# The sixteen gate columns of a first projection: split f32r products replaced by f32 products in four column groups, one block ahead

## The chip, the cores and the metric

The kernel runs on one core of a Trainium2 chip. Its time is device microseconds of one execution; a kernel is judged by the median of its runs. One execution was also taken by the profiler, and all rows below come from that one.

## The reference: what is computed

One layer of a streaming encoder on a prompt of 4096 frames and 8 running streams of 16 new frames (128 sample rows). Only the beginning matters here:

```
xn   = rms_norm(h, ln_g)                     # 1024 columns
proj = xn @ w_in
qkv_a, a_raw, b_raw, ... = split(proj)       # 1536 | 8 | 8 | ...
conv = silu(depthwise causal conv, width 4, of qkv_a)
beta = sigmoid(b_raw)
g    = -exp(a_log) * softplus(a_raw + dt_bias)
gc   = cumsum(g) within blocks of 64 frames
```

The sixteen columns a_raw and b_raw are the gate columns. The delta rule, an attention over a band of frames, an output projection and an embedding follow.

## The kernel before

The kernel is a sequence of stages, each with its own buffers and semaphores and a barrier at its end. The first is `project_a` (line 110), which makes the 1536 columns of qkv_a and the 16 gate columns; the second, `project_b`, makes the other columns and reads back what the first has stored. Each engine has its own program, written out by hand in `project_a`, and runs it in order; semaphores (`wait_ge`, `then_inc`) are the only links.

**Tiling.** The 4096 prompt frames and 128 sample rows are 33 row tiles of 128. A block b is two tiles, 256 frames, so there are 16 full blocks, and block 16 holds the sample tile alone. Each tile is squared and scaled on ACT, transposed on PE (`transposes`), multiplied by ln_g on DVE into `x_full` (two buffers), and split into a high f32r part on ACT (`split_hi`) and the rest on DVE (`split_lo`). The tiles of block b+1 are prepared during block b: the first around groups 0 to 4, the second around groups 5 to 9.

**Products.** The 1536 columns are twelve groups g of 128. A group is a `product` (line 484): for each of 8 slices of the 1024 rows, three f32r matmuls (`matmul3`, lines 86 to 90: high by high, low by high, high by low), 24 in all, into one of four PSUM banks `psG`. After the twelve groups of a block the gate columns are a thirteenth `product` of 24 matmuls with 16 columns of weights, into columns 0 to 255 of the bank `psAB` (line 533). The weights themselves arrive in 32 pieces in block 0 and before, and are split likewise: the high part on ACT (`hi_part`), the low part alternately on DVE and POOL (`lo_part`, line 214). In block 0 group 9 waits for pieces 24 to 31.

**Behind the products.** ACT copies each group into one of six `raw` buffers (line 438), DVE convolves it with four instructions (lines 573 and 576), and ACT applies SiLU (line 394). For block b-1, PE makes four key-query products during block b, one behind each of the groups 0 to 3 (`keys_queries`, line 501); each goes into the one bank `psK`, must be copied by ACT (`take_kq`, line 401, one of two `kq` buffers) before the next, and is stored by SP (`store_kq`, line 240). `take_kq` for the third waits until the stores of the first have landed. Behind group 5 PE makes the query sums in columns 256 to 511 of `psAB` (`query_sums`, line 509).

**Gate arithmetic.** `decays(b)` (line 578) is at the end of DVE's block b: it adds dt_bias to the gate product, and ten more steps on 16x256 tiles, most of which wait for the one before, give gc and beta. ACT's part, two exponentials and a logarithm (lines 464 to 468), is at the end of ACT's block. Both engines go on to the next block's groups only behind it.

**Queue.** SP issues every DMA of the stage in order. In block b it stores the key-query products of b-1, loads and stores row tiles, then `store(b)` (line 249): it waits for the last SiLU, stores the block, waits for the end of `decays(b)`, and stores gc and beta with four DMAs (line 256).

Of the kernel before, what the change touches and what calls it, by code (L numbers as in the profile page):

```python
# [26 lines left out]
F32R = mybir.dt.float32r  # L27
ACT = mybir.ActivationFunctionType
ALU = mybir.AluOpType
AX = mybir.AxisListType  # L30

P = 128
# [77 lines left out]
def project_a(nc, d, s):  # L110
# [4 lines left out]
    G = QKV // P  # L115
    HA, N, HALO, TAPS = s.HA, 2 * P, s.CONVW - 1, s.CONVW
    C = s.DV
    WCOLS = QKV + 2 * HA
    PAIRS = HA // 2
    RING, SLOTS = 6, 7  # L120
    CUTS = [0, 3 * P, 6 * P, 9 * P, WCOLS]
    PIECES = [(k, CUTS[i], CUTS[i + 1]) for i in range(4) for k in range(KT)]
    WIDEST = max(b - a for k, a, b in PIECES)
    HALVES = len(PIECES) // 2
    with ExitStack() as stack:
        ph = Phase(nc, stack)
        w_hi = ph.sb("a_w_hi", [P, KT, WCOLS], F32R)
        w_lo = ph.sb("a_w_lo", [P, KT, WCOLS], F32R)
        x_raw = [ph.sb(f"a_x{i}", [P, D]) for i in range(2)]
        squares = ph.sb("a_squares", [P, D], mybir.dt.bfloat16)  # L130
        x_full = [ph.sb(f"a_x_full{i}", [P, KT, P]) for i in range(2)]
# [7 lines left out]
        ssq_rows = ph.sb("a_ssq_rows", [P, N])  # L139
        pair_ones = ph.sb("a_pair_ones", [P, 32])  # L140
        taps = ph.sb("a_taps", [P, TAPS, G])
        lnT = ph.sb("a_lnT", [P, KT])
        ident = ph.sb("a_ident", [P, P])
        ssq = ph.sb("a_ssq", [P, 2])
# [16 lines left out]
        psK = ph.ps("a_psK", [P, 512])  # L161

        ln_in = ph.sem("a_ln_in")
        consts = ph.sem("a_consts")
        filled = ph.sem("a_filled")
        cleared = ph.sem("a_cleared")
# [31 lines left out]
        stored = [ph.sem(f"a_stored{i}") for i in range(2)]  # L198
        ab_stored = ph.sem("a_ab_stored")
        last_rows = ph.sem("a_last_rows")  # L200
        V_AB, S_AB = 11, 3

        stage = [act[1][:, :, :].rearrange("p g n -> p (g n)")[:, i * WIDEST:(i + 1) * WIDEST] for i in range(SLOTS)]

        def tiles_of(b):
            return range(2 * b, min(2 * b + 2, TILES))
# [16 lines left out]
        def _(sp):  # L223
# [6 lines left out]
            def spill(t):  # L230
                sp.wait_ge(full_ok, t + 1)
                sp.dma_start(d.xT[t], x_full[t % 2][:, :, :]).then_inc(spilled[t % 2], 16)
# [16 lines left out]
            def store(b):  # L249
                sp.wait_ge(silu, G * (b + 1))  # L250
                sp.dma_start(d.qkvB[b], act[b % 2][:, :, :]).then_inc(stored[b % 2], 16)
                sp.wait_ge(ab_v, V_AB * (b + 1))
                n = N // C
                for x, there in ((gc[0:HA, :], d.gcC), (beta[HA:2 * HA, :], d.betaC)):
                    for e in range(2):
                        sp.dma_start(there[n * b:n * (b + 1), e * PAIRS:(e + 1) * PAIRS].rearrange("n h i -> h n i"),
                                     x[e::2, :].rearrange("h (n i) -> h n i", n=n)).then_inc(ab_stored, 16)
# [5 lines left out]
            for m, (k, a, b) in enumerate(PIECES):  # L263
                if m >= SLOTS:
                    weights_ready(sp, m - SLOTS + 1)
                sp.dma_start(stage[m % SLOTS][:, 0:b - a], d.w_in[k * P:(k + 1) * P, a:b]).then_inc(w_in[m % SLOTS], 16)
                if m == 5:
                    with nc.allow_non_contiguous_dma(reason="small per-channel constants, once"):
                        for j in range(TAPS):
                            sp.dma_start(taps[:, j, :], d.conv_w[j, :].rearrange("(g p) -> p g", p=P)).then_inc(consts, 16)  # L270
                        sp.wait_ge(cleared, 2)
                        sp.dma_start(dt_b[0:HA, :], d.dt_bias.rearrange("(h o) -> h o", o=1)).then_inc(consts, 16)
                        sp.dma_start(alog[0:HA, :], d.a_log.rearrange("(h o) -> h o", o=1)).then_inc(consts, 16)
                if m == 16:
                    load_x(2)
                    spill(0)
                if m == 20:
                    load_x(3)
                    spill(1)
            for b in range(BLOCKS + 1):  # L280
                if b:
                    for f in range(4):
                        store_kq(b - 1, f)
                for t in tiles_of(b + 1):
                    if t + 2 < TILES:
                        load_x(t + 2)
                    spill(t)
                    if b and t % 2 == 0:
                        store_rows(b - 1)
                if b == BLOCKS:  # L290
                    store_rows(b - 1)
                else:
                    store(b)
            with nc.allow_non_contiguous_dma(reason="three columns, once"):
                sp.wait_ge(halo_ok, G * BLOCKS)
                sp.dma_start(d.lastT.rearrange("(g p) t -> p g t", p=P), halo[:, :, :]).then_inc(last_rows, 16)
# [71 lines left out]
        def _(e):  # L368
# [10 lines left out]
            def split_hi(t):  # L379
                b, a = t // 2, t % 2  # L380
                e.wait_ge(full_ok, t + 1)
                if b >= 2:
                    e.wait_ge(grp_ok, G * (b - 1))
                    e.wait_ge(ab_ok, b - 1)
                e.activation(xT_hi[b % 2][:, :, a * P:(a + 1) * P], x_full[a][:, :, :], ACT.Copy).then_inc(hi_ok, 1)

            def hi_part(m):
# [15 lines left out]
            def take_rows(b):  # L403
                e.wait_ge(rows_ps, b + 1)
                if b:
                    e.wait_ge(rows_out, 16 * PAIRS * b)
                e.activation(ssq_rows[:, :], psAB[:, N:], ACT.Copy).then_inc(rows_ok, 1)

            square(0)
            square(1)  # L410
# [12 lines left out]
            for b in range(BLOCKS + 1):  # L423
                ahead = list(tiles_of(b + 1))
                for g in range(G):
# [29 lines left out]
                    if len(ahead) > 1:  # L455
                        if g == 5:
                            square(ahead[1])
                        if g == 6:
                            scale(ahead[1])
                        if g == 9:  # L460
                            split_hi(ahead[1])
                if b < BLOCKS:
                    conv_silu(b, G - 1)
                e.wait_ge(ab_v, V_AB * b + 3)
                e.activation(u[:, :], na[:, :], ACT.Exp).then_inc(ab_s, 1)
                e.activation(en[:, :], xa[:, :], ACT.Exp, scale=-1.0).then_inc(ab_s, 1)
                e.wait_ge(ab_v, V_AB * b + 4)
                e.activation(ln_w[:, :], w[:, :], ACT.Ln).then_inc(ab_s, 1)

        @block.tensor  # L470
        def _(pe):
# [10 lines left out]
            def product(out, cols, b, n, first):  # L482
# [4 lines left out]
                                   xT_lo[b % 2][:, k, 0:n], k == 0, k == KT - 1)  # L487
                return last

            def keys_queries(b, f):  # L490

                a, x = f // 2, act[b % 2]
                n = 4 * b + f
                pe.wait_ge(silu, G * b + 2 * PAIRS)
                if n:
                    pe.wait_ge(kq_ok, n)
                rows_e = slice(f % 2 * C, (f % 2 + 1) * C)
                for p in range(PAIRS):
                    for c2 in range(2):
                        at = slice(a * P + c2 * C, a * P + (c2 + 1) * C)  # L500
                        last = nc.tensor.matmul(psK[c2 * C:(c2 + 1) * C, p * 2 * C:(p + 1) * 2 * C], x[rows_e, PAIRS + p, at],
                                                x[rows_e, p:p + PAIRS + 1:PAIRS, at], start=True, stop=True)
                last.then_inc(kq_ps, 1)

            def query_sums(b):
                pe.wait_ge(qsq_ok, b + 1)
                pe.wait_ge(ab_v, V_AB * b + 1)
                for p in range(PAIRS):
                    last = nc.tensor.matmul(psAB[32 * p:32 * (p + 1), N:], pair_ones[:, :], qsq[:, p, :], start=True, stop=True)
                last.then_inc(rows_ps, 1)  # L510
# [3 lines left out]
            for b in range(BLOCKS + 1):  # L514
# [3 lines left out]
                for g in range(G):  # L518
# [5 lines left out]
                        keys_queries(b - 1, g)  # L524
                    if b and g == 5:
                        query_sums(b - 1)
                    if g == 3 and ahead:
                        transposes(ahead[0])
                    if g == 8 and len(ahead) > 1:
                        transposes(ahead[1])  # L530
                if b:
                    pe.wait_ge(rows_ok, b)
                product(psAB[0:2 * HA, 0:n], slice(QKV, WCOLS), b, n, None).then_inc(ab_ok, 1)

        @block.vector
        def _(v):
# [11 lines left out]
            def full(t):  # L548
                v.wait_ge(xT_ps, t + 1)
                if t >= 2:  # L550
                    v.wait_ge(spilled[t % 2], 16 * (t // 2))
                    v.wait_ge(lo_ok, t - 1)
                v.tensor_tensor(x_full[t % 2][:, :, :], psT[:, :].rearrange("p (k n) -> p k n", k=KT),
                                lnT[:, :].unsqueeze(2).to_broadcast([P, KT, P]), ALU.mult).then_inc(full_ok, 1)

# [22 lines left out]
            def decays(b, gates):  # L578
                at = V_AB * b
                n = P * len(tiles_of(b))  # L580
                v.wait_ge(ab_ok, b + 1)
                v.tensor_scalar(xa[:, 0:n], psAB[0:2 * HA, 0:n], dt_b[:, :], None, ALU.add).then_inc(ab_v, 1)
                v.wait_ge(ab_v, at + 1)
                v.tensor_scalar(nx[:, :], xa[:, :], -1.0, None, ALU.mult).then_inc(ab_v, 1)
                v.wait_ge(ab_v, at + 2)
# [33 lines left out]
            for b in range(BLOCKS):  # L619
# [3 lines left out]
                for g in range(G):  # L623
# [8 lines left out]
                        full(ahead[1])  # L632
                    if g == 9 and len(ahead) > 1:
                        split_lo(ahead[1])
                decays(b, gate)
            decays(BLOCKS, gate_s)


GROUPS = 4
# [2618 lines left out]
```

## Time and profile before

| | |
|---|---|
| Median of 3 runs | 3945.96 us (3920.86 to 3954.39) |
| Profiled execution, its own time | 3943.41 us |
| Its span | 3941.6 us |
| Mean granted TensorE clock | 0.945 |
| Busy: PE, DVE, ACT, POOL | 3548.4, 2212.2, 1299.6, 1018.9 us |
| `project_a` | 0 to 803.8 us |

Busy time is the share in which an engine had an instruction running. Matmuls are pipelined, so the start-to-start spacing, not the duration, is what one costs. A line number is that of kernel.py; a helper's line covers all its callers. SPq is SP's DMA queue.

### The profile page before, as it was taken

What the parts mean: (1) busy time and instruction counts of PE and PEld (TensorE: products, weight loads), DVE (VectorE), ACT (ScalarE), POOL (GpSimd) and SP (SyncE); (2) the same over time, 40 slices, a digit from 0 to 9 for tenths busy, and PEclk for the clock granted to TensorE, in tenths of its full rate; (3) what the DMA queues carried; (4) which work ended last, traced back from release to release, by engine and by line L of the source; (5) the groups of instructions that cost most, each with busy time, mean ns of one, the idle gap of its engine ahead of it and who ended that gap; (6) DMA issues with size and microseconds to landing.
All of it is one profiled execution on the core that took longest, in us unless ns stands there. A gap on an engine that the chain in (4) does not pass through costs nothing. (4 is left out here: it accounts for less than half of the span.)

```text
span 3941.6 us, 68538 instructions
## 1 busy us (share of the span) xinstructions
PE 3548.4 (90%) x26510; PEld 3020.0 (77%) x26510; DVE 2212.2 (56%) x4204; ACT 1299.6 (33%) x2368; POOL 1018.9 (26%) x1284
## 2 busy tenths in 40 slices
PE   7999999979996898995777569999977999999999
PEld 6999999967885686874676467888854788888887
DVE  7777777357974758681466436666633423333332
ACT  5455444232222323211233206666622211111111
POOL 4222222057983525400577600000000000000000
PEclk9999999889998899997899779999988999999999
DMA  5333433244334333333999522222244312112120
GB/s 157 104 118 101 115 100 102 60 147 158 115 112 140 118 116 116 111 109 79 211 231 233 131 62 92 77 73 81 84 117 167 106 59 69 64 57 69 65 67 34
DMA packets 380768, 426.62 MB, mean 108 GB/s; under 512 B 188267, under 2 KB 271499, under 8 KB 377918
## 3 DMA queue, kind: packets, MB, share of 16 engines
q1 hardware_dynamic: 380486, 422.80, 37.8%
q8 instruction: 185, 3.03, 0.3%
q14 instruction: 97, 0.79, 0.1%
HBM read 265.09 MB, written 160.25 MB: 108 GB/s over the span
## 5 line engine op out<-in xcount | busy, mean ns | idle before, releaser
L88 PE MATMUL b_psP<-b_w_hi,b_xT_hi 128*128 128x512 f32 x1320 | 525.5, 398 | 105.8 <-DVE b_xT_lo L1180 89.0
L89 PE MATMUL b_psP<-b_w_lo,b_xT_hi 128*128 128x512 f32 x1320 | 522.6, 396 | 0.0
L90 PE MATMUL b_psP<-b_w_hi,b_xT_lo 128*128 128x512 f32 x1320 | 521.6, 395 | 0.0
L88 PE MATMUL a_psG<-a_xT_hi,a_w_hi 128*128 128x256 f32 (+1 forms) x1632 | 475.0, 291 | 10.3 <-DVE a_xT_lo L559 9.4
L90 PE MATMUL a_psG<-a_xT_hi,a_w_lo 128*128 128x256 f32 (+1 forms) x1632 | 467.0, 286 | 0.0
L89 PE MATMUL a_psG<-a_xT_lo,a_w_hi 128*128 128x256 f32 (+1 forms) x1632 | 466.8, 286 | 0.0
L88 PEld LDWEIGHTS b_psP<-b_w_hi,b_xT_hi 128*128 128x128 f32 x1320 | 253.5, 192 | 166.1 <-DVE b_xT_lo L1180 112.8
L88 PEld LDWEIGHTS a_psG<-a_xT_hi,a_w_hi 128*128 128x128 f32 x1632 | 316.5, 194 | 26.6 <-DVE a_xT_lo L559 9.8
L576 DVE SCALAR_TENSOR_TENSOR a_act<-a_raw,a_taps,a_act 128x256 f32<-128x256 f32 x576 | 308.7, 536 | 20.5
L90 PEld LDWEIGHTS a_psG<-a_xT_hi,a_w_lo 128*128 128x128 f32 x1632 | 317.1, 194 | 0.0
L89 PEld LDWEIGHTS a_psG<-a_xT_lo,a_w_hi 128*128 128x128 f32 x1632 | 316.7, 194 | 0.0
L90 PEld LDWEIGHTS b_psP<-b_w_hi,b_xT_lo 128*128 128x128 f32 x1320 | 253.3, 192 | 53.8
L89 PEld LDWEIGHTS b_psP<-b_w_lo,b_xT_hi 128*128 128x128 f32 x1320 | 253.6, 192 | 52.6
L2516 DVE CUSTOM_DVE_ANT_0 f_neg<-f_score,f_bias 128x640 f32<-128x640 f32 (+4 forms) x256 | 192.4, 780 | 83.5 <-PE f_score L2416 55.2
L3000 POOL TENSOR_SCALAR h_var<-h_ssq 128x1 f32<-128x1 f32 x33 | 6.3, 190 | 870.8 <-ACT h_squares L3032 870.8
L88 PE MATMUL h_psH<-h_w_hi,h_mT_hi 128*128 128x512 f32 x528 | 209.2, 396 | 6.7 <-DVE h_w_lo L107 6.7
L1180 DVE TENSOR_TENSOR b_xT_lo<-b_x_full,b_xT_hi 128x1024 fp32r<-128x1024 f32 x72 | 105.7, 1468 | 186.2 <-ACT b_xT_hi L1095 186.2
L900 DVE TENSOR_TENSOR b_tmp_v<-b_M,b_col_v 128x62 f32<-128x62 f32 (+28 forms) x464 | 205.9, 484 | 3.5
L1143 ACT ACTIVATE b_rows<-b_psP 128x512 f32<-128x512 f32 x99 | 58.8, 598 | 451.5 <-PE b_psP L90 316.7
L2335 ACT ACTIVATE f_prob<-f_neg,f_low 128x640 f32<-128x640 f32 (+4 forms) x256 | 201.2, 788 | 17.9 <-DVE f_low L2516 17.9
L90 PE MATMUL h_psH<-h_w_hi,h_mT_lo 128*128 128x512 f32 x528 | 206.4, 391 | 0.0
L89 PE MATMUL h_psH<-h_w_lo,h_mT_hi 128*128 128x512 f32 x528 | 206.4, 391 | 0.0
(378 smaller groups left out, 7707.8 us busy)
## 6 DMA issues: line engine op xcount, KB each, us to landing
rows_b<-b_rows SPq DMA_DIRECT2D x165, 256.0 KB, 2.1
b_x_full<-xT SPq DMA_DIRECT2D x72, 512.0 KB, 4.1
qkvB<-a_act SPq DMA_DIRECT2D x16, 1536.0 KB, 5.1
d_conv_T<-qkvB SPq DMA_DIRECT2D x32, 768.0 KB, 5.8
xT<-a_x_full SPq DMA_DIRECT2D x33, 512.0 KB, 5.1
h_mixed<-mixed SPq DMA_DIRECT2D x33, 512.0 KB, 4.0
out<-h_y SPq DMA_DIRECT2D x33, 512.0 KB
a_x<-in_x_prompt SPq DMA_DIRECT2D x32, 512.0 KB, 4.4
```

Of the source, the lines that this page charges most:

```text
L88: nc.tensor.matmul(out, x_hi, w_hi, start=first, stop=False)
L89: nc.tensor.matmul(out, x_hi, w_lo, start=False, stop=False)
L90: return nc.tensor.matmul(out, x_lo, w_hi, start=False, stop=last)
L576: v.scalar_tensor_tensor(out, x[:, j:j + N], taps[:, j, g:g + 1], out, ALU.mult, ALU.add).then_inc(conv, 1)
L900: eng.tensor_tensor(t, U[:, c0:c1, j:j + 1].to_broadcast([P, c1 - c0, L]), factor.unsqueeze(1).to_broadcast([P, c1 - c0, L]), ALU.mult).th ...
L1143: e.activation(rows[u % ROWS][:, :], psP[u % BANKS][:, :], ACT.Copy if seg == V else ACT.Silu).then_inc(taken, 1)
L1180: v.tensor_tensor(xT_lo[n % XBUFS][:, :, :], x_full[n % 2][:, :, :], xT_hi[n % XBUFS][:, :, :].bitcast(F32), ALU.subtract).then_inc(lo_ok, 1)
L2335: e.activation(prob[h % 4][:, 0:n], neg[h % 2][:, 0:n], ACT.Exp, scale=-1.0, bias=low[a.b][:, h:h + 1], accum_out=total[a.b][:, h:h + 1]). ...
L2516: v.tensor_tensor_reduce(neg[h % 2][:, 0:n], score[h % 2][:, 0:n], bias[:, h, KEYS - n:], -1.0 / ROOT, BIG, ALU.add, ALU.min, low[a.b][:, ...
L3000: g.tensor_scalar(var[:, :], ssq[:, :], 1.0 / D, EPS, ALU.mult, ALU.add).then_inc(e_var, 1)
```

## The change

The gate columns leave the split f32r weights. They get a tile of their own, `w_ab`, 32 columns wide in f32 (the 16 gate columns and the 16 behind them, of which the results are not used), loaded once at weight piece 12. A function `gates(t)` on PE multiplies one row tile in f32 from `x_full`: eight products of 128 streamed columns, of which product q of each four writes the partitions 32q to 32q+15 (and 16 unused) of `psAB`, so that the eight slices of the contraction add up in four parts. DVE adds the four parts with three new adds. All of it is done one block ahead: PE calls `gates` for the tiles of block b+1 behind groups 9 and 11 of block b (and for tiles 0 and 1 behind group 2 of block 0); `decays(b + 1)` stands where `decays(b)` stood, and `decays(0)` behind group 5 of block 0; SP stores the gates of b+1 behind the block b.

```diff
-    WCOLS = QKV + 2 * HA
+    PARTS, PCOLS = 4, 32
-    CUTS = [0, 3 * P, 6 * P, 9 * P, WCOLS]
+    CUTS = [0, 3 * P, 6 * P, 9 * P, QKV]
+        w_ab = ph.sb("a_w_ab", [P, KT, PCOLS])
-        V_AB, S_AB = 11, 3
+        V_AB, S_AB = 10 + PARTS, 3
 # SP
             def store(b):
                 sp.wait_ge(silu, G * (b + 1))
                 sp.dma_start(d.qkvB[b], act[b % 2][:, :, :]).then_inc(stored[b % 2], 16)
+
+            def store_gates(b):
                 sp.wait_ge(ab_v, V_AB * (b + 1))
...
+                if m == 12:
+                    sp.dma_start(w_ab[:, :, :], d.w_in[:, QKV:QKV + PCOLS].rearrange("(k p) c -> p k c", p=P)).then_inc(w_ab_in, 16)
...
+            store_gates(0)
             for b in range(BLOCKS + 1):
...
                     store(b)
+                    if b + 1 < BLOCKS:
+                        store_gates(b + 1)
 # ACT
-                    e.wait_ge(ab_ok, b - 1)
...
+            def decays(b):
+                e.wait_ge(ab_v, V_AB * b + PARTS + 2)
+                (the same two exponentials; wait for + PARTS + 3; the same logarithm)
...
+                    if b == 0 and g == 5:
+                        decays(0)
                 if b < BLOCKS:
                     conv_silu(b, G - 1)
-                e.wait_ge(ab_v, V_AB * b + 3)
-                (two exponentials, wait, logarithm)
+                    decays(b + 1)
 # PE
+            def gates(t):
+                b, at = t // 2, slice(t % 2 * P, (t % 2 + 1) * P)
+                pe.wait_ge(full_ok, t + 1)
+                if t == 0:
+                    pe.wait_ge(w_ab_in, 16)
+                if b:
+                    pe.wait_ge(ab_v, V_AB * (b - 1) + PARTS)
+                if b >= 2:
+                    pe.wait_ge(rows_ok, b - 1)
+                for k0 in range(0, KT, PARTS):
+                    for q in range(PARTS):
+                        last = nc.tensor.matmul(psAB[PCOLS * q:PCOLS * (q + 1), at], w_ab[:, k0 + q, :], x_full[t % 2][:, k0 + q, :],
+                                                start=k0 == 0, stop=k0 + PARTS == KT)
+                last.then_inc(ab_ok, 1)
...
-                pe.wait_ge(ab_v, V_AB * b + 1)
+                pe.wait_ge(ab_v, V_AB * (b + 1) + PARTS)
...
+                    if b == 0 and g == 2:
+                        gates(0)
+                        gates(1)
+                    if g == 9 and ahead:
+                        gates(ahead[0])
+                    if g == G - 1 and len(ahead) > 1:
+                        gates(ahead[1])
...
-                if b:
-                    pe.wait_ge(rows_ok, b)
-                product(psAB[0:2 * HA, 0:n], slice(QKV, WCOLS), b, n, None).then_inc(ab_ok, 1)
 # DVE
                 if t >= 2:
...
+                    v.wait_ge(ab_ok, t - 1)
...
-                v.wait_ge(ab_ok, b + 1)
+                v.wait_ge(ab_ok, tiles_of(b)[-1] + 1)
                 v.tensor_scalar(xa[:, 0:n], psAB[0:2 * HA, 0:n], dt_b[:, :], None, ALU.add).then_inc(ab_v, 1)
+                for q in range(1, PARTS):
+                    v.wait_ge(ab_v, at + q)
+                    v.tensor_tensor(xa[:, 0:n], xa[:, 0:n], psAB[PCOLS * q:PCOLS * q + 2 * HA, 0:n], ALU.add).then_inc(ab_v, 1)
...
+                    if b == 0 and g == 5:
+                        decays(0, gate)
-                decays(b, gate)
-            decays(BLOCKS, gate_s)
+                decays(b + 1, gate if b + 1 < BLOCKS else gate_s)
```

## Rows read from the trace of the kernel before

**Rows 1.** Busy time by stretch: us, PE, PEld, DVE, ACT, POOL, PEclk, DMA, GB/s
```profile
158.75:202.84 44.09, 44.09 (x403) 41.84 (x401) 32.88 (x63) 22.11 (x44) 10.97 (x29) 1.00 0.38 109
749.00:790.00 41.00, 41.00 (x203) 39.90 (x199) 0.00 (x0) 2.81 (x9) 0.00 (x0) 0.51 0.10 14
```

**Rows 2.** Waits of PE, 110 to 700 us: us in total, times, longest us
```profile
PE a_psK L501 <- ACT a_kq L401: 2.0, 4, 0.8
```

**Rows 3.** Timeline of PE, blocks 2 and 3: start, us, engine, line, op, tiles
```profile
156.03 0.28 PE L88 MATMUL a_psAB<-a_xT_hi,a_w_hi 128*16 128x256 f32 x1
...
158.64 0.28 PE L90 MATMUL a_psAB<-a_xT_hi,a_w_lo 128*16 128x256 f32 x1
...
169.79 1.09 PE L501 MATMUL a_psK<-a_act 64*64 64x128 f32 x16
...
173.85 1.09 PE L501 MATMUL a_psK<-a_act 64*64 64x128 f32 x16
...
200.12 0.28 PE L88 MATMUL a_psAB<-a_xT_hi,a_w_hi 128*16 128x256 f32 x1
```

**Rows 4.** Timeline of DVE across the same end of a block
```profile
157.03 1.52 DVE L576 SCALAR_TENSOR_TENSOR a_act<-a_raw,a_taps,a_act 128x256 f32<-128x256 f32 x3
158.95 0.47 DVE L582 TENSOR_SCALAR a_xa<-a_psAB,a_dt 16x256 f32<-16x256 f32 x1 [0.39 <-PE a_psAB L90]
159.46 0.28 DVE L584 TENSOR_SCALAR a_softplus<-a_xa 16x256 f32<-16x256 f32 x1
...
166.71 0.24 DVE L573 TENSOR_SCALAR a_act<-a_raw,a_taps 128x256 f32<-128x256 f32 x1
```

**Rows 5.** Timeline of SP's queue, the same stretch
```profile
166.81 1.34 SPq L256 DMA_DIRECT2D gcC<-a_gc  x2
...
169.46 7.41 SPq L240 DMA_DIRECT2D kq<-a_kq  x8
```

**Rows 6.** Timeline of ACT, the same stretch
```profile
160.32 0.42 ACT L465 ACTIVATE a_u<-a_na 16x256 f32<-16x256 f32 x1
...
168.88 0.58 ACT L401 ACTIVATE a_kq<-a_psK 128x512 f32<-128x512 f32 x1
...
172.88 0.60 ACT L401 ACTIVATE a_kq<-a_psK 128x512 f32<-128x512 f32 x1 [1.80 <-DMA kq<-a_kq]
```

**Rows 7.** Timeline of PE around f32 products (x4: window cut short)
```profile
93.19 0.28 PE L90 MATMUL a_psG<-a_xT_hi,a_w_lo 128*128 128x256 f32 x1
93.40 0.64 PE L509 MATMUL a_psAB<-a_qsq,a_pair_ones 128*32 128x256 f32 x8
...
94.19 0.28 PE L89 MATMUL a_psG<-a_xT_lo,a_w_hi 128*128 128x256 f32 x1
...
93.40 0.42 PE L509 MATMUL a_psAB<-a_qsq,a_pair_ones 128*32 128x256 f32 x4
...
71.20 1.09 PE L501 MATMUL a_psK<-a_act 64*64 64x128 f32 x16
```

**Rows 8.** A PSUM tile as operand on DVE: ns min/median/max, first and last start
```profile
L3116 DVE TENSOR_TENSOR h_pT_lo<-h_psE,h_pT_hi x33: 411/412/416, 3077.1 to 3918.2; 128x256 fp32r<-128x256 f32 x33
```

**Rows 9.** Timeline of DVE and PE in block 0
```profile
52.88 0.34 DVE L573 TENSOR_SCALAR a_act<-a_raw,a_taps 128x256 f32<-128x256 f32 x1
...
58.97 0.39 PE L88 MATMUL a_psG<-a_xT_hi,a_w_hi 128*128 128x256 f32 x1 [0.89 <-DVE a_w_lo L217]
```

**Rows 10.** Timeline of SP's queue at the end of the stage
```profile
791.11 0.38 SPq L298 DMA_DIRECT2D rawT_s<-a_act  x1
...
803.81 0.36 SPq L920 DMA_DIRECT2D b_x_full<-xT  x1
```

**Rows 11.** DMA from 791 to 804 us, in 40 slices
```profile
GB/s 0 0 0 217 296 284 296 284 296 285 295 167 0 0 0 0 0 0 0 0 0 0 0 0 0 0 0 0 0 0 0 0 0 13 13 0 0 0 0 0
```

**Rows 12.** Timeline of PE at its first wide products
```profile
26.75 0.58 PE L88 MATMUL a_psG<-a_xT_hi,a_w_hi 128*128 128x256 f32 x1 [9.42 <-DVE a_xT_lo L559]
...
29.48 0.41 PE L88 MATMUL a_psG<-a_xT_hi,a_w_hi 128*128 128x256 f32 x1
```

More of the change, by code:

```diff
@@ L126, in project_a @@
         ph = Phase(nc, stack)
-        w_hi = ph.sb("a_w_hi", [P, KT, WCOLS], F32R)
-        w_lo = ph.sb("a_w_lo", [P, KT, WCOLS], F32R)
+        w_hi = ph.sb("a_w_hi", [P, KT, QKV], F32R)
+        w_lo = ph.sb("a_w_lo", [P, KT, QKV], F32R)
         x_raw = [ph.sb(f"a_x{i}", [P, D]) for i in range(2)]
@@ L163, in project_a @@
         ln_in = ph.sem("a_ln_in")
+        w_ab_in = ph.sem("a_w_ab_in")
         consts = ph.sem("a_consts")
@@ L407, in take_rows @@
                 e.activation(ssq_rows[:, :], psAB[:, N:], ACT.Copy).then_inc(rows_ok, 1)
+            def decays(b):
+                e.wait_ge(ab_v, V_AB * b + PARTS + 2)
+                e.activation(u[:, :], na[:, :], ACT.Exp).then_inc(ab_s, 1)
+                e.activation(en[:, :], xa[:, :], ACT.Exp, scale=-1.0).then_inc(ab_s, 1)
+                e.wait_ge(ab_v, V_AB * b + PARTS + 3)
+                e.activation(ln_w[:, :], w[:, :], ACT.Ln).then_inc(ab_s, 1)
             square(0)
@@ L461, in _ @@
                             split_hi(ahead[1])
+                    if b == 0 and g == 5:
+                        decays(0)
                 if b < BLOCKS:
                     conv_silu(b, G - 1)
-                e.wait_ge(ab_v, V_AB * b + 3)
[L465 to L468, printed above, removed]
+                    decays(b + 1)
         @block.tensor
@@ L580, in decays @@
                 n = P * len(tiles_of(b))
-                v.wait_ge(ab_ok, b + 1)
+                v.wait_ge(ab_ok, tiles_of(b)[-1] + 1)
                 v.tensor_scalar(xa[:, 0:n], psAB[0:2 * HA, 0:n], dt_b[:, :], None, ALU.add).then_inc(ab_v, 1)
+                for q in range(1, PARTS):
+                    v.wait_ge(ab_v, at + q)
+                    v.tensor_tensor(xa[:, 0:n], xa[:, 0:n], psAB[PCOLS * q:PCOLS * q + 2 * HA, 0:n], ALU.add).then_inc(ab_v, 1)
+                at += PARTS - 1
                 v.wait_ge(ab_v, at + 1)
```

## The prediction, made before the changed kernel was run

> **What bounds the kernel now.** The change touches only the first stage, project_a, which ends near 803.8 us of the 3941.6 us span, so I read that stage. First the busy time by stretch: one full block (two row tiles, 256 frames) lasts 44.09 us, and in it PE is busy for all 44.09, DVE for 32.88, ACT for 22.11, with a granted clock of 1.00 [rows 1]. PE looks like the only bound. Then the waits of PE: between 110 and 700 us, 2.0 us in all, each of them for ACT's copy of a key-query product, a_kq [rows 2]. They are few, but the same copy is what becomes late if anything else slips, so I followed one block through PE, DVE, ACT and SP in order of time.
>
> I call E the moment at which PE has started the last of a block's twelve wide groups and begins the gate product: E = 156.03. The gate product is 24 instructions, the last at 158.64. The next block's third key-query product starts at 169.79, its fourth at 173.85, and the next E is 200.12 [rows 3]. So a period is 17.82 us (E to the fourth product) plus 26.27 us (from there to the next E).
>
> Beside the first part runs a chain that the gate product does not set. DVE ends the twelfth convolution at 158.55, that is E + 2.5; starts the gate arithmetic at 158.95 after a wait of 0.39; and begins the next convolution at 166.71 [rows 4]. SP cannot store the gates before that: its issues run from 166.81, and the key-query stores queued behind them from 169.46 [rows 5]. ACT may reuse its copy buffer only when the first of these stores has landed, so its third copy starts at 172.88 after a wait of 1.80 for that DMA and ends at 173.48; its second copy, held by the first convolution after the gate arithmetic, ends at 169.46 [rows 6]. PE needs them at 173.85 and 169.79: the slack is 0.37 and 0.33 us. So in each block two bounds lie within 0.4 us of each other: PE's own work, and the chain E, twelfth convolution, gate arithmetic, SP's gate stores, key-query store, ACT copy. The 2.7 us of gate product run in the shadow of that chain.
>
> **The change part by part.**
>
> Removed on PE: the 24 narrow instructions between E and the next block. They go from 156.03 to 158.75 (158.64 and one spacing of 0.11): 2.72 us [rows 3].
>
> Added on PE: two calls of gates per block, each 8 f32 products of 32 columns on 128 rows, streaming 128. The query sums are the nearest kind (32 columns, four column groups): 4 products appear as 8 records. The first four records together last 0.42 us while a single one lasts 0.40, so the four groups run side by side. From the last wide record before them (93.19) to the second after (94.19) is 1.00 us where 0.24 is normal, two spacings of 0.12: 0.76 us for 8 x 256 streamed columns [rows 7]. A call of gates has 16 records x 128 columns, the same total: I take 0.8 us. The upper end is the key-query product, 16 records x 128 columns in two column groups, which lasts 1.09 [rows 7] and costs about 1.2 with the same entry and exit. I take 0.8 because width, group count and streamed columns match the sums. The page "TensorE: Matmul & The Clock Gate" of the Trainium skill (What happens when you issue a matmul) says that, without hardware decode, each matmul instruction costs about 62 ns of sequencer time; by that a call would be 16 x 62 = 1.0 us and 0.2 of entry, 1.2 in all. The four starts within 0.02 us speak against it here.
>
> Where these calls lie matters. The first sits behind group 9, inside the 26.27 us, where nothing waits: +0.8 per block on the period. The second sits behind E, in the shadow of the chain: nothing. If the chain were gone, both would count, with the 2.72 saved.
>
> Added on DVE: three adds of a 16x256 PSUM part, each waiting for the one before. An add with one PSUM operand on 256 columns lasts 0.41 [rows 8]; dependent steps of this arithmetic follow each other every 0.50 us (158.95 to 159.46) [rows 4]. I take 0.50 each, 1.5 in all; ends are 0.41 each without a gap and 0.65. Against it stands the 0.39 wait for the gate product, which goes, and about 0.1 with which unrelated DVE instructions overlap: the arithmetic can start at about E + 2.45. Net delay of its end against E: 1.5 - 0.5 = +1.0 us (0.7 to 1.5). ACT's exponential now starts at 160.32 [rows 6], right behind its input, so it moves along.
>
> Queued behind it: on DVE the next block's convolutions, on ACT the next group's copies, on SP four gate stores and then the key-query stores. All end 1.0 later against E. The fourth product then starts at E + 17.45 + 1.0 + 0.15 = E + 18.6, where PE alone would be ready at E + 0.8 + 15.1 = E + 15.9. So E to the fourth product grows from 17.82 to 18.6, and PE now waits some 2.7 us per block before the second, third and fourth products. Per period: +0.8 (chain) +0.8 (first call) = **+1.6 us**, for the 14 periods between the fourth product of block 1 and that of block 15: **+22.4**. The gates of the last, half-wide tile need adds of 128 columns, about 0.35 each: +0.5 and again +0.8, **+1.3**.
>
> Block 0: it now does the arithmetic twice, once behind group 5 and once at its end. The added one takes the 7.76 us from 158.95 to 166.71 plus 1.5, that is 9.3 us, on DVE before the convolution that now starts at 52.88. DVE shows no idle time from there on, and the low parts of the weights for groups 9 to 11 are queued behind: PE already waits 0.89 for them at 58.97 [rows 9]. Nothing covers it: +9.3. Then the block's ordinary arithmetic is 1.5 longer, of which about 0.6 is hidden by ACT's table load: +0.9. The two calls for tiles 0 and 1 vanish in PE's wait. Together **+10.2** (7 to 12).
>
> SP: its gate stores move from the block's own to the next one's values, same number and place. The extra load of the 16 columns at weight piece 12 is one issue of perhaps 1.5 us at a time when SP waits for DVE: nothing, up to 1. In block 0 the loads of tile 4 come some 15 us later, and its rows are used only in block 1.
>
> The end of the stage: E of the last block, the gate product, DVE's arithmetic, two stores, and the next stage's first load is issued at 803.81. After the change only the copy of rawT_s is left, issued at 791.11; its bytes flow until slice 12 of 40 in the window from 791 to 804, that is 794.9 [rows 10, 11]. Nothing else is open, so the next stage starts near 795.3: **-8.5** (-7 to -9).
>
> Sum: 22.4 + 1.3 + 10.2 - 8.5 = **+25.4 us**. The profiled execution took 3943.4, so 3968.8; it stands 2.6 below the median of the three runs, whose spread is 33 us. I predict 3970.
>
> **The rivals.**
> 1. The saving reaches the end. If the chain did not hold PE, a period would lose 2.72 - 1.6 = 1.1 us: 16 x 1.1 = 18 less, 8.5 less at the end, 10.2 more in block 0: -16, 3927, and -26, 3917, if DVE's doubled arithmetic in block 0 were covered too. It decides only if the fourth product can start before E + 17.0, that is if the arithmetic ended 0.5 us earlier against E than now; with three more adds it cannot, and the four waits of PE in [rows 2] show the chain already touching. Chance 0.06.
> 2. The new waits lower TensorE's clock. Before its first wide product PE stood 9.42 us; that product and those up to 29.48 last 0.41 and more where 0.28 is usual, the half clock (1.2 GHz) by their length: 2.7 us at half speed, 1.4 lost [rows 12]. In the last, half-wide block the granted clock fell to 0.51 with PE never idle [rows 1]. If each block's three waits (0.8, 1.9, near 0) did this once: 15 x 1.4 = +21, 3990. Against: a block has waited before, and from 158.75 to 202.84 the clock was 1.00. The same page of the Trainium skill (HAM oscillation) says that a product stream broken by waits falls back to half clock again and again, which is this case; no row here shows it. Chance 0.14.
> 3. Everything dear: a call of gates at 1.2 (+0.4 per period) and adds at 0.65 (+0.45): +13, and block 0 at 12: 3984. Chance 0.15.
> 4. The forecast, +18 to +33: 0.65.
>
> **How the numbers follow.** Likeliest 3970. The range goes from 3946 (adds and block 0 at their low ends: +15, less 12 for the scatter of a median of such runs) to 4000 (rivals 2 and 3 with some scatter). One per cent, 39 us, is about what a measurement of this kernel can tell from no change. The forecast case lies under it in most of its width (0.54 of 0.65), rival 3 by half, rival 2 hardly; rival 1 is within it except for scatter: faster 0.03, same 0.70, slower 0.27.
>
> **What would show it.** In the profile after: PE idle before the second and third key-query products, 1 to 2 us each, released by ACT a_kq; periods between fourth products of 45.5 to 46 us where they are 44.1; gates as 16 records in about 0.55 us, and the adds 0.50 apart; 8 to 10 us of PE idle in block 0 before group 9's last weights, released by DVE a_w_lo; the next stage's first load within 5 us of the last ACT copy. Wrong if PE's idle time in blocks 2 to 15 stays under 0.5 us per block (then the chain does not hold, rival 1), if the granted clock falls under 0.95 there (rival 2), or if block 0 gives back what the arithmetic costs it.

## The result, and the profile after

The changed kernel takes 3993.24 us (median of 6, 3983.42 to 4007.91) where the kernel before takes 3944.49 (3920.86 to 3954.39): ratio 1.0136, 95% interval 1.0099 to 1.0173. It is slower by 49 us; 25 were forecast for the likeliest case.

The whole difference lies in project_a. The next stage's first load, at 803.81 before [rows 10], is at 852.46, 48.65 later. The profiled execution of the changed kernel took 4007.9 us, 64.5 more than the profiled one before: some 16 us of that lie behind this stage. The medians differ by 48.75 us, so I take those 16 us as scatter between executions; that is not shown.

Timeline of PE in block 3 of the changed kernel, the counterpart of [rows 3] (start, us, then as before):

```profile
163.78 0.28 PE L90 MATMUL a_psG<-a_xT_hi,a_w_lo 128*128 128x256 f32 x1
163.99 0.65 PE L515 MATMUL a_psAB<-a_x_full,a_w_ab 128*32 128x128 f32 x16
...
164.79 0.28 PE L89 MATMUL a_psG<-a_xT_lo,a_w_hi 128*128 128x256 f32 x1
...
170.50 0.65 PE L515 MATMUL a_psAB<-a_x_full,a_w_ab 128*32 128x128 f32 x16
...
178.82 1.09 PE L530 MATMUL a_psK<-a_act 64*64 64x128 f32 x16 [0.53 <-ACT a_kq L409]
...
184.76 1.09 PE L530 MATMUL a_psK<-a_act 64*64 64x128 f32 x16 [1.79 <-ACT a_kq L409]
...
186.47 0.28 PE L90 MATMUL a_psG<-a_xT_hi,a_w_lo 128*128 128x256 f32 x1
186.59 0.38 PE L88 MATMUL a_psG<-a_xT_hi,a_w_hi 128*128 128x256 f32 x1
186.77 0.42 PE L89 MATMUL a_psG<-a_xT_lo,a_w_hi 128*128 128x256 f32 x1
...
190.34 1.09 PE L530 MATMUL a_psK<-a_act 64*64 64x128 f32 x16
```

E is 170.39 here. The two new waits stand before the second and third key-query products, and 1.8 us after the third begins the wide products go over from 0.12 to 0.21 us apart. The third starts at E + 14.4, where 14.6 follows from the forecast's chain. The fourth starts at E + 19.95; in the period in which the clock stays up and no further wait is added it starts at E + 18.5, where 18.6 was forecast. Below are the waits of PE from 120 to 740 us, where [rows 2] had 2.0 us from 110 to 700, and the granted clock (PEclk, third from the end) in the stretch of the slow products, in the next, and in the last block:

```profile
PE a_psK L530 <- ACT a_kq L409: 31.5, 29, 1.8
```

```profile
138.80:142.20 3.40, 3.40 (x18) 3.40 (x18) 1.70 (x4) 0.76 (x2) 0.41 (x2) 0.51 0.84 147
142.30:183.00 40.70, 40.15 (x375) 37.77 (x374) 30.05 (x57) 18.63 (x37) 9.71 (x27) 1.00 0.34 105
790.00:845.00 55.00, 55.00 (x274) 53.17 (x274) 0.82 (x1) 4.16 (x13) 0.00 (x0) 0.50 0.11 16
```

DVE and SP behind the twelfth convolution, against [rows 4, 5]:

```profile
172.86 0.47 DVE L616 TENSOR_SCALAR a_xa<-a_psAB,a_dt 16x256 f32<-16x256 f32 x1
173.36 1.32 DVE L619 TENSOR_TENSOR a_xa<-a_xa,a_psAB 16x256 f32<-16x256 f32 x3
174.72 0.28 DVE L622 TENSOR_SCALAR a_softplus<-a_xa 16x256 f32<-16x256 f32 x1
...
181.88 0.24 DVE L607 TENSOR_SCALAR a_act<-a_raw,a_taps 128x256 f32<-128x256 f32 x1
```

```profile
181.97 1.34 SPq L260 DMA_DIRECT2D gcC<-a_gc  x2
...
184.62 5.31 SPq L242 DMA_DIRECT2D kq<-a_kq  x6
```

The three adds take 1.36 us. The arithmetic starts at E + 2.5, and the next convolution at E + 11.5, 0.8 later against E than before.

PE in block 0, and the end of the stage:

```profile
61.37 0.90 PE L492 MATMUL a_psT<-a_ident,a_x 128*128 128x128 f32 x3 [5.49 <-ACT a_x L386]
61.41 0.24 DVE L607 TENSOR_SCALAR a_act<-a_raw,a_taps 128x256 f32<-128x256 f32 x1
```

```profile
846.68 0.39 SPq L307 DMA_DIRECT2D rawT_s<-a_act  x1
847.11 0.68 SPq L309 DMA_DIRECT2D gcT<-a_gc  x1
847.83 1.12 SPq L310 DMA_DIRECT2D betaT<-a_beta  x1
852.46 0.35 SPq L959 DMA_DIRECT2D b_x_full<-xT  x1
```

By the starts of the fourth key-query products the 48.65 us divide up:

| from | to | before | after | difference | forecast |
|---|---|---|---|---|---|
| start | block 1 | 85.70 | 95.79 | +10.1 | +10.2 |
| block 1 | block 15 (14 periods) | 619.48 | 657.55 | +38.1 | +22.4 |
| block 15 | block 16 | 42.98 | 48.67 | +5.7 | +1.3 |
| block 16 | rawT_s | 42.95 | 44.67 | +1.7 | 0 |
| rawT_s | next stage | 12.70 | 5.78 | -6.9 | -8.5 |

Of the 14 periods, the ten in which the clock fell last 47.26 to 47.29 us; the four others last 46.18, 45.77, 46.82 and 46.03. The waits before the second and third products are the same in all 14 (0.52 to 0.54 and 1.77 to 1.79 us), so their length does not tell why the clock fell in ten. Three of the four others have one more wait for a_kq, of 0.18 to 0.99 us, before the fourth product; the kernel before has such odd waits in four periods too, and its 14 periods last 44.25 on average.

### The profile page after: what moved, and what is told of

Same layout as the page of the kernel before. It is cut to its first block and busy times, and to the rows that moved or that the text cites. A ratio compares the mean times of both kernels' runs of the same rounds, so it can differ in the third digit from the quotient of the medians.

```text
span 4006.1 us, 68894 instructions
## 1 busy us (share of the span) xinstructions
PE 3573.1 (89%) x26630; PEld 3040.2 (76%) x26630; DVE 2228.1 (56%) x4255; ACT 1296.2 (32%) x2369; POOL 1007.7 (25%) x1284
## 5 line engine op out<-in xcount | busy, mean ns | idle before, releaser
L88 PE MATMUL a_psG<-a_xT_hi,a_w_hi 128*128 128x256 f32 (+1 forms) x1632 | 493.6, 302 | 9.5 <-DVE a_xT_lo L593 9.4
L89 PE MATMUL a_psG<-a_xT_lo,a_w_hi 128*128 128x256 f32 (+1 forms) x1632 | 480.7, 295 | 0.0
L90 PE MATMUL a_psG<-a_xT_hi,a_w_lo 128*128 128x256 f32 (+1 forms) x1632 | 480.1, 294 | 0.0
L88 PEld LDWEIGHTS a_psG<-a_xT_hi,a_w_hi 128*128 128x128 f32 x1632 | 332.1, 204 | 32.7 <-issue 11.7
L89 PEld LDWEIGHTS a_psG<-a_xT_lo,a_w_hi 128*128 128x128 f32 x1632 | 332.8, 204 | 0.0
L90 PEld LDWEIGHTS a_psG<-a_xT_hi,a_w_lo 128*128 128x128 f32 x1632 | 332.7, 204 | 0.0
L610 DVE SCALAR_TENSOR_TENSOR a_act<-a_raw,a_taps,a_act 128x256 f32<-128x256 f32 x576 | 309.3, 537 | 20.5
L88 PE MATMUL h_psG<-h_w_hi,h_hT_hi 128*128 128x512 f32 x528 | 205.7, 390 | 0.0
```

The lines of the kernel that those rows point to most:

```text
L88: nc.tensor.matmul(out, x_hi, w_hi, start=first, stop=False)
L89: nc.tensor.matmul(out, x_hi, w_lo, start=False, stop=False)
L90: return nc.tensor.matmul(out, x_lo, w_hi, start=False, stop=last)
L610: v.scalar_tensor_tensor(out, x[:, j:j + N], taps[:, j, g:g + 1], out, ALU.mult, ALU.add).then_inc(conv, 1)
```

## The experiments

All ratios are to the kernel before on the same chip; medians of kernels measured on different chips are compared only roughly. Periods are between fourth key-query products; the stage end is the next stage's first load.

| kernel | median, us | ratio (95%) | usual period | clock falls, blocks 2 to 15 | stage end |
|---|---|---|---|---|---|
| before | 3944.49 | 1 | 44.09 | none | 803.8 |
| after | 3993.24 | 1.0136 (1.0099 to 1.0173) | 47.27 | 10 | 852.5 |
| fill | 3975.25 | 1.0075 (1.0044 to 1.0106) | 45.77 | none | 841.4 |
| no_adds | 3967.10 | 1.0070 (1.0046 to 1.0094) | 45.0 or 46.5 | 6 | 829.4 |
| one_slice | 3958.72 | 1.0042 (1.0017 to 1.0066) | 43.9 to 47.0 | 9 | 824.1 |
| three_steps | 3967.66 | 1.0072 (1.0052 to 1.0092) | 45.12 | none | 822.7 |
| late | 3919.37 | 0.9952 (0.9926 to 0.9978) | 43.98 | none | 777.2 |
| late0 | 3915.48 | 0.9946 (0.9922 to 0.9971) | 43.98 | none | 775.0 |
| before_late | 3918.03 | 0.9955 (0.9931 to 0.9979) | 44.09 | none | 777.4 |
| last_fill | 3922.39 | 0.9958 (0.9938 to 0.9978) | 44.09 | none | 783.3 |
| late3 | 3907.84 | 0.9918 (0.9886 to 0.9950) | 43.36 | none | 768.3 |
| late3_pitch | 3908.94 | 0.9919 (0.9890 to 0.9949) | 43.14 | none | 763.3 |
| late3_shift | 3905.49 | 0.9908 (0.9875 to 0.9942) | 43.36 | none | 768.5 |

**fill**: do the waits lower the clock, or the f32 products?

```diff
+                    if b and g in FILL:        # FILL = {1: 4, 2: 12}
+                        pe.wait_ge(evac, G * b + g - 2)
+                        for _ in range(FILL[g]):
+                            nc.tensor.matmul(psG[(g + 1) % 4][:, 0:n], w_hi[:, 0, (g + 1) * P:(g + 2) * P],
+                                             xT_hi[b % 2][:, 0, 0:n], start=True, stop=True)
```

> The changed kernel, but PE does not stand idle before the key-query products: 4 extra wide products before the second and 12 before the third of each block (about 0.5 and 1.4 us of streaming, into a PSUM bank that the next group resets). The results are unchanged, there is only more work. Theory (the waits lower TensorE's clock): the granted clock stays 1.00 in blocks 2 to 15, the period falls from 47.3 to 45.8 us, the stage ends 15 to 25 us sooner than in the changed kernel, the kernel is 0.4 to 0.6% faster than the changed one (about 3973, +0.7% on before). Rival (the f32 products in column groups lower the clock, or the length of the period is work on PE): the clock keeps falling once per block, periods stay 47.3 or grow by up to 1.9 us: 3993 to 4020.

```profile
110.00:720.00 610.00, 600.80 (x5611) 567.67 (x5610) 454.12 (x872) 285.46 (x568) 135.20 (x385) 1.00 0.36 103
```

The window's row has the clock at 1.00 with more work done. The usual period is 45.77, the forecast's 45.7; five of the 14, with an odd wait of 0.54 to 1.17 us, are longer, and the 14 together last 645.4 us where the changed kernel's last 657.6: 12.2 less. The stage ends 11 us earlier, less than expected, since in block 16 the clock fell again, at 775.5, and its period came out 1.9 longer than in the changed kernel. The f32 products in column groups do not lower the clock; the waits do.

**no_adds**: the changed kernel with its `for q in range(1, PARTS)` loop replaced by `v.sem_inc(ab_v, PARTS - 1)`. It leaves out three of the four parts of each gate.

> The changed kernel without the three adds: only the first of the four parts enters the gates (this part of the computation is left out), everything else in its place. Theory (the chain from the last group over DVE's gate arithmetic to the ACT copies sets the fourth key-query product): the arithmetic ends 1.36 us sooner, all of it reaches PE while it still waits (2.3 us per block now): period 45.8 - 1.3 = 44.5, and since the third product's wait shrinks to about 0.5 us the clock may hold 1.00, which gives 1.5 more against 47.3. Stage end 35 to 45 us before that of the changed kernel; 3950 to 3960. Rival (adds are hidden beside PE): period unchanged at 47.3, 3993.

```profile
132.95 1.09 PE L530 MATMUL a_psK<-a_act 64*64 64x128 f32 x16 [1.62 <-ACT a_kq L409]
```

The period is 45.0 instead of the expected 44.5 where the clock holds, and the clock falls in six periods. The stage ends 23 us before that of the changed kernel, not 35 to 45. The adds reach PE, but only 0.8 of their 1.36 us: with them gone, ACT's exponential waits for its table load again, which in the kernel before ends at 160.31, just before the start in [rows 6]. The rival, no change, is out. In blocks 2 to 15 there is one wait of 1.6 us before the third product here, and none before the second: one such wait is enough for the clock to fall in some blocks.

**one_slice**: the kernel before with an eighth of the gate product; the other seven slices are left out.

```diff
-                product(psAB[0:2 * HA, 0:n], slice(QKV, WCOLS), b, n, None).then_inc(ab_ok, 1)
+                matmul3(nc, psAB[0:2 * HA, 0:n], w_hi[:, 0, QKV:WCOLS], w_lo[:, 0, QKV:WCOLS], xT_hi[b % 2][:, 0, 0:n],
+                        xT_lo[b % 2][:, 0, 0:n], True, True).then_inc(ab_ok, 1)
```

> The kernel before with 3 instead of 24 narrow gate products per block (7 of 8 slices of the contraction are left out), everything else in its place. Theory (the gate product runs in the shadow of the chain): E to the fourth key-query product can shrink only by the slack, so the period goes from 44.09 to about 43.5, not to 41.7; PE begins to wait about 1.8 us per block for a_kq, and the clock may fall as in the changed kernel, which would make it 44 to 45. Time between -10 and +15 us on before. Rival (PE's work is the bound): period 41.7, 2.4 us less in each of 16 blocks, -40 us, 3905.

```profile
PE a_psK L501 <- ACT a_kq L401: 29.1, 28, 1.8
```

This is the sharpest of them: 2.4 us less PE work per block make the kernel slower (1.0042). PE now waits 29.1 us between 120 and 700 us, and the clock falls in nine periods. Of the five periods without a fall, three last 43.9, only 0.2 less than before, and two, with a further wait of 1.0 us, last 45.0.

**three_steps**: the kernel before, with 1.36 us more on DVE alone.

```diff
+                for q in range(1, 4):
+                    v.wait_ge(ab_v, at + q)
+                    v.tensor_tensor(xa[:, 0:n], xa[:, 0:n], xa[:, 0:n], ALU.min).then_inc(ab_v, 1)
```

> The kernel before with three extra dependent 16x256 steps on DVE behind the first of the gate arithmetic (minimum of a tile with itself; results unchanged), 0.45 us each; PE, ACT and SP do the same as before. Theory: 1.36 us on a chain with 0.35 us of slack gives +1.0 per period, 45.1, with the clock at 1.00 if waits of about 1 us do not lower it: +15 to +17 us, 3960; with a fall of the clock in most blocks up to +38. Rival (DVE's steps are hidden, PE is the bound): no change, 3944.

```profile
172.40 1.09 PE L501 MATMUL a_psK<-a_act 64*64 64x128 f32 x16 [0.97 <-ACT a_kq L401]
```

The usual period grows by 1.03 us, as expected, and this wait of 0.97 us does not lower the clock in a full block. In four periods a second wait of 0.28 to 1.17 us follows within 6 us, and there the clock stays up too.

**late, late0, before_late**: only the steps that read PSUM stay at the block's end. Late and late0 start from the changed kernel, before_late from the kernel before. On DVE (on ACT and SP alike; in before_late `finish(b - 1)`):

```diff
                 for g in range(G):
                     convolve(b, g)
...
+                    if g == 5:
+                        finish(b, gate)        # the ten steps behind the PSUM reads
-                decays(b + 1, gate if b + 1 < BLOCKS else gate_s)
+                gather(b + 1)                  # the four steps that read psAB
```

> The changed kernel, but of the gate arithmetic only the four steps that read the PSUM bank stay at the end of a block; the other ten (with ACT's three activations, and SP's gate stores) move behind group 5 of the next block, where no key-query product follows. Block 0 keeps its full arithmetic behind group 5. Theory (the arithmetic hurts only by its place ahead of the key-query copies): PE no longer waits, clock 1.00, period 44.09 - 2.72 + 1.6 = 43.0; fourth key-query product of block 1 about 5 us later than before, stage end near 782 us where the kernel before has 803.8 and the changed one 852.5; 3920 to 3925, 0.5% faster than before, 1.8% faster than the changed kernel. Rival (DVE or ACT now make PE wait elsewhere, or the f32 products cost more than 1.6 us per block): periods of 44 us and more, 3940 or above.

> As late, and in block 0 the PSUM reads stand behind group 7 (after the last low part of the weights) and the rest at the block's end. Theory (block 0's cost is DVE time ahead of the weights' low parts): PE no longer idles before groups 8 and 9, the fourth key-query product of block 1 comes 2 us after that of the kernel before instead of 5, stage end near 779; 0.1% faster than late. Rival (block 0 is bound elsewhere): no difference in stage end.

> The kernel before (f32r gate product at the end of its block), with only the order of the arithmetic changed: the first step that reads PSUM stays, the other ten move behind group 5 of the next block. Theory: PE is as busy as before, so periods stay 44.09, less the odd longer one (four of them, 0.3 to 0.9 us), and block 1 loses its 2.2 us of waits; stage end 798 to 802, the time within 0.2% of before. So the f32 products' own worth is the 1.1 us per period by which late is shorter than this. Rival (the order alone gives the gain): stage end as in late.

From 110 to 720 us all three have no wait for a_kq, and they are about 0.5% faster than before; but half of what was expected of them is wrong. before_late, with the old products, ends its stage 26 us sooner, not 2 to 6. And late's period is 43.98, not 43.0. PE's waits in late, 110 to 720 us:

```profile
PE a_psG L88 <- DVE a_xT_lo L590: 8.2, 14, 0.6
```

DVE, put back at group 5, finishes the next block's second tile 0.6 us late. Late0 ends its stage 2.2 us before late, which agrees in sign with block 0's cost, but late0 still waits 3.9 us for a_kq in block 1.

**last_fill**: the kernel before, with eight products more in the last block. Where did before_late's 26 us come from? 19.2 of them lie between the fourth product of block 16 and rawT_s (42.95 before, 23.74 there).

```diff
+                    if b == BLOCKS and g == 3:
+                        pe.wait_ge(evac, G * b + g - 2)
+                        for _ in range(8):
+                            nc.tensor.matmul(psG[0][:, 0:n], w_hi[:, 0, 4 * P:5 * P], xT_hi[b % 2][:, 0, 0:n], start=True, stop=True)
```

> The kernel before, with 8 extra half-wide products in the last block before its fourth key-query product, where PE otherwise stands idle for 0.55 us; results unchanged, no work removed. In before, the clock halves 2 us after that wait and the last block's groups take 5.12 us; in before_late, without the wait, it stayed up until 770 us. Theory (the short wait tips the clock in a block whose products stream only 128 columns): the clock stays at 1.00 for most of the last block, the stage ends some 15 to 20 us sooner, 784 to 789, the kernel about 0.4% faster than before. Rival (the half-wide block loses the clock anyway, the wait is a coincidence): stage end 804, no change.

The same window of before and of last_fill:

```profile
749.00:770.00 21.00, 21.00 (x109) 19.90 (x106) 0.00 (x0) 1.43 (x4) 0.00 (x0) 0.53 0.15 26
```

```profile
749.00:770.00 21.00, 21.00 (x191) 20.49 (x190) 0.00 (x0) 2.82 (x9) 0.00 (x0) 1.00 0.19 27
```

Eight useless products take 20.5 us off the stage, 803.8 to 783.3, as expected. In before, this was the wait, and the first of the slow products behind it:

```profile
748.16 1.09 PE L501 MATMUL a_psK<-a_act 64*64 64x128 f32 x16 [0.55 <-ACT a_kq L401]
...
750.13 0.40 PE L90 MATMUL a_psG<-a_xT_hi,a_w_lo 128*128 128x128 f32 x1
```

**late3**: late0 with `if b and g == 3` for the ten steps.

> As late0, but in blocks 1 to 16 the ten steps of the arithmetic stand behind group 3 instead of group 5. In late PE waits 0.6 us at each block's start for the low part of the second tile, because DVE, put 7 us back at group 5, is busy without a pause until then; so the period was 43.98 and the f32 products' 1.1 us did not show. Theory (DVE's backlog at groups 5 to 9 is what holds PE): behind group 3 the idle time of groups 4 to 7 takes it up, no wait for a_xT_lo, period 43.0 to 43.2, stage end 761 to 764, 3901 to 3905, 1.0% faster than before. Rival (the period is bound by something else, or the f32 products cost PE 2.6 us): 43.9, stage end 775, 3916.

```profile
165.48:208.88 43.40, 43.40 (x409) 40.91 (x408) 33.87 (x67) 22.30 (x43) 10.74 (x29) 1.00 0.39 111
```

PE has no wait from 110 to 720 us. The kernel is 0.8% faster than before and 2.1% under the changed kernel by the medians, but its stage end of 768.3 is later than the 761 to 764 expected, and the period of 43.36 is 0.4 above the sum, 44.09 - 2.72 + 1.55 = 42.92. Most of the gain on before is that of before_late, 26 of the 35 us of stage end; the f32 products with the place behind group 3 bring the other 9. No run has the old products with that place, but before_late has no wait of PE in its full blocks that the place could take away.

**late3_pitch, late3_shift**: the row pitch of the weight tiles.

```diff
-        w_hi = ph.sb("a_w_hi", [P, KT, QKV], F32R)
+        w_hi = ph.sb("a_w_hi", [P, KT, QKV + 2 * HA], F32R)
```

(w_lo is changed alike; late3_shift instead puts an unused [P, 128] tile behind each of the two.)

> As late3, with the two tiles of wide weights as wide as before the change (1552 columns instead of 1536, the last 16 unused). In every kernel with the narrower tiles the wide products start 0.1197 us apart, in every kernel with the old ones 0.1182: 288 x 0.0015 = 0.44 us per block, just what late3's period of 43.36 lacks to 42.92. Theory (the row pitch of the weight tiles costs PE this): spacing 0.1182, period 42.9, stage end 761 to 762, 3901, 0.17% faster than late3. Rival (the spacing comes from the products of the f32 kind or from other tiles' places): 0.1197 and 43.36 as in late3.

> As late3, pitch 1536, but with two unused tiles of 128 columns behind the two weight tiles, so that all tiles lie where they lie in late3_pitch. If the pitch counts, the spacing stays 0.1197; if only the places of the tiles count, it is 0.1182 here too.

The mean spacing of the wide products in one period is 0.1181 us in late3_pitch, 0.1197 in late3 and in late3_shift, 0.1182 in before: the pitch, not the place. The period falls by 0.22, not 0.44, and the stage ends 5.1 us sooner; the time does not tell the three apart. The other 0.2 is a wait that late3 does not have. ACT's scaling of the next tile (L387) does not come sooner with PE, and in late3_pitch the transposes of that tile wait for it, about 0.25 us once per block. From 110 to 720 us:

```profile
PEld a_psT L494 <- ACT a_x L387: 3.4, 13, 0.3
```

## Why the prediction was right, and where it was not

**The number.** 3993 lies in the range up to 4000, but not in the forecast's own case of +18 to +33; it lies in the range because that was stretched for rivals 2 and 3, and next to rival 2's 3990. Of the 48.65 us in the stage, 25.4 are the sum's and 23.3 are not: 15.7 in the 14 periods, 6.1 in the last block and 1.6 at the end of the stage.

**The bound** was read rightly: the chain through the gate arithmetic lay within 0.4 us of PE's work. one_slice and three_steps show it from both sides.

**The sizes on PE and DVE** held: a call of gates costs 0.77 (163.78 to 164.79, less 0.24), not the 1.2 of its upper end; the adds 0.45 each instead of 0.50, the chain +0.8 instead of +1.0. The usual period without a fall of the clock, 45.77 in fill, meets the forecast's 45.7.

**Block 0** came to +10.1 against +10.2, and that is luck. The wait named was the wrong one: PE stood 5.49 us for ACT's scaling of the second tile, queued behind ACT's part of the arithmetic, before it came to the weights, and not 8 to 10. About 4.4 us of the rest are the clock again, which the forecast had at 1.00 here. It fell from 60.3 to 67.2 us, of which 5.8 had PE busy, worth about 2.9 us by my estimate, and once more in block 1, worth 1.5 as in the later blocks. The first row has the first of these stretches, the second the other (PEclk 0.51):

```profile
60.30:67.20 6.90, 5.81 (x26) 5.51 (x26) 6.69 (x12) 3.22 (x7) 4.88 (x6) 0.51 0.23 40
91.00:94.50 3.50, 3.50 (x20) 3.19 (x17) 1.81 (x4) 1.30 (x4) 0.42 (x2) 0.51 0.86 150
```

The two calls for tiles 0 and 1 did not vanish either: from the first product of the third group to that of the fourth, block 0 takes 3.98 us (33.49 to 37.47) where it took 2.84.

**The step that failed** is the clock: the sum took it at 1.00, with the fall as rival 2 at 0.14, priced at 1.4 us each. The price was right (47.27 - 45.77 = 1.5), the chance too low: it fell in ten of 14 periods. By fill, which has no fall there, this is 12.2 of the 15.7 us that the 14 periods took too many; that is less than ten times 1.5, because the odd waits before the fourth product, which come in some periods, do not show where the clock has fallen. The other 3.5 are in fill too, whose periods last 46.10 on average, where 44.25 + 1.6 = 45.85; most of this is odd waits, more than before. The reason given against the fall was weak: from 158.75 to 202.84 us PE did not wait at all, and the waits in [rows 2] were at most 0.85 us long. Only one of 1.70, at 81.04 us in block 1, had passed without a fall. After the change every full block has one of 1.8. fill shows that the waits are the cause by taking most of them away, and no_adds that a single one of 1.6 us is enough. Why the same waits lower the clock in one block and not in the next stays open. The page "TensorE: Matmul & The Clock Gate" of the Trainium skill (HAM oscillation) describes a kernel that waits after each stretch of products and starts each next stretch at the low clock. Here the trace agrees in kind, with waits of 1.8 us and in ten of 14 periods, not in all.

**The last block** was taken at +1.3 and cost +7.4: 5.7 up to its fourth product and 1.7 from there to rawT_s. It loses the clock in both kernels, from 750 us before and 787 after; after the change it does so earlier in the block, so the third and fourth products come late too. I had read 0.51 in [rows 1] as a fall without a wait, because the window began at 749: the wait of 0.55 us ended just before it, at 748.16.

**The end of the stage** gave 6.9 of 8.5: the prediction had left nothing behind rawT_s, but two small stores queue behind it on SP (847.11, 847.83), and the next load comes 5.8 us after rawT_s instead of 4.2. By the landings in the trace rawT_s is complete at 850.8 and the small stores at 851.15, 0.35 later. From there to the next load pass 1.3 us, as they did before (802.54 to 803.81); the sum had left that step out.

Rival 1, the saving reaching the end, was rightly excluded here; late3 is the kernel in which it happens. There the products bring 44.09 - 43.36 = 0.73 us per period over before_late. The wider spacing at the pitch of 1536 columns, 288 x 0.0015 = 0.43 us per period, is a cost that no step of the prediction had; taking it away gave back 0.22, since PE then meets ACT's scaling.

## What to carry to other kernels

Before removing work from the busiest engine, follow one period through all engines: a chain with 0.3 us of slack turns the saving into a wait, and a step added to that chain costs all but the slack. A wait of PE can have two prices, itself and the clock afterwards; if it cannot be removed, filling it with throwaway products can pay. That a stretch without waits ran at full clock says nothing about the clock with them, and one wait that passed without a fall is no safe sign: the same wait lowered the clock in ten blocks here and not in four others. Work that is ready a block ahead should also be moved off the place where everyone waits for it, or being ahead buys nothing.

## What the runs showed of the hardware

A PE wait of 0.55 us, in a block whose products stream 128 columns, was followed 2 us later by half clock for the rest of the block; with the wait filled the products ran on at 1.00 beyond 770 us. In blocks with 256 columns a wait of 0.97 us did nothing (three_steps), a single one of 1.6 lowered it in six of 14 periods (no_adds), and 0.53 followed by 1.79 in ten of 14 (after); such a fall cost 1.5 us (47.27 against 45.77). Two other waits of that length passed without a fall: 1.70 us in block 1 of before and 1.84 in block 1 of three_steps. The spacing of f32r products of 256 columns with 128 weight columns was 0.1181 to 0.1182 us at a weight row pitch of 1552 words (late3_pitch, before) and 0.1197 at 1536 (late3, late3_shift). Four column groups of f32 products ran side by side, 16 records of 128 columns in 0.65 us.
